# First projections of a hybrid transformer layer: fp32 matmuls over all tokens become three fp32r passes over two token halves

## The reference, cut to what matters

```python
qa, ka, va, za, aa, ba, ub, qn, kn, vn, gr = split_cols(h @ w_in)
...
qkv = jax.nn.silu(short_conv(jnp.concatenate([q, k, v], axis=-1), conv_w))
q = l2norm(q.reshape(b_, t_, GDN_HEADS, GDN_DK))
k = l2norm(k.reshape(b_, t_, GDN_HEADS, GDN_DK))
if rotary:
    q = axial_rope(q)
    k = axial_rope(k)
...
return (rmsnorm(o, norm_w) * jax.nn.silu(zh)).reshape(b_, t_, GDN_V_W)
```

## Time and profile before

| | |
|---|---|
| median of 3 runs | 3821.11 us |
| lowest, highest | 3817.90, 3821.98 us |
| the profiled execution: own time | 3825.0 us |
| its span | 3823.5 us |
| mean granted clock of TensorE | 0.977 |
| TensorE busy | 3659.4 us, 96% |
| VectorE, ScalarE, GpSimd busy | 2323.0, 1645.7, 856.0 us |

### The profile page before, as it was taken

How to read it: one execution, slowest core, us unless ns; L and a number is a source line. 1 busy time by engine, 2 the same in 40 slices (tenths; PEclk the granted TensorE clock), 3 DMA queues, 4 the chain that set the end, 5 groups by cost and what they waited for, 6 DMA issues and landing times. The chain is left out here.

```text
span 3823.5 us, 58042 instructions
## 1 busy us (share of the span) xinstructions
PE 3659.4 (96%) x19520; PEld 2936.9 (77%) x19520; DVE 2323.0 (61%) x3546; ACT 1645.7 (43%) x3006; POOL 856.0 (22%) x812
## 2 busy tenths in 40 slices
PE   8999999999997999989999999996799999999998
PEld 3444459986777999968888888785688888888887
DVE  4655632555656999953534353444767777677775
ACT  4333333334654666642424332322344445444452
POOL 3888500011106666610000000000000010000100
PEclk9999999999999999989999999997899999999999
DMA  7455455131115433344535352443477676766763
GB/s 283 155 144 142 119 182 130 57 86 45 26 46 183 125 118 122 96 160 125 177 105 170 99 172 73 152 154 130 145 214 226 214 220 206 214 224 215 219 209 92
DMA packets 258768, 570.97 MB, mean 149 GB/s; under 512 B 38971, under 2 KB 117339, under 8 KB 256347
## 3 DMA queue, kind: packets, MB, share of 16 engines
q1 hardware_dynamic: 225612, 451.18, 37.2%
q0 software_dynamic: 33040, 118.25, 10.4%
HBM read 458.27 MB, written 100.73 MB: 146 GB/s over the span
## 5 line engine op out<-in xcount | busy, mean ns | idle before, releaser
L3072 DVE TENSOR_TENSOR sb_we_low<-sb_we,sb_we_high 128x1024 fp32r<-128x1024 f32 x384 | 466.6, 1223 | 121.5 <-ACT sb_we_high L3023 121.5
L3023 ACT ACTIVATE sb_we_high<-sb_we 128x1024 fp32r<-128x1024 f32 x377 | 392.2, 1048 | 142.3 <-PE ey L2987 142.3
L2430 DVE TENSOR_TENSOR sb_wm_low<-sb_wm,sb_wm_high 128x1024 fp32r<-128x1024 f32 x127 | 155.4, 1224 | 393.6 <-ACT sb_wm_high L2340 393.6
L344 PE MATMUL p_ps<-sb_hT,sb_ring 128*128 128x512 f32 (+1 forms) x960 | 373.2, 549 | 0.0
L344 PEld LDWEIGHTS p_ps<-sb_hT,sb_ring 128*128 128x128 f32 x960 | 181.9, 190 | 186.2 <-issue 181.3
L2281 PE MATMUL pg<-sb_hb_high,sb_wm_high 128*128 128x512 f32 x768 | 303.3, 395 | 8.7 <-DVEq L2402 4.6
L2282 PE MATMUL pg<-sb_hb_low,sb_wm_high 128*128 128x512 f32 x768 | 300.4, 391 | 0.0
L2283 PE MATMUL pg<-sb_hb_high,sb_wm_low 128*128 128x512 f32 x768 | 300.1, 391 | 0.0
L2970 PE MATMUL eg<-sb_xe_parts,sb_we_high 128*128 128x512 f32 x1024 | 260.5, 396 | 1.6 <-DVE sb_xe_parts L3067 1.6
L2970 PE MATMUL eu<-sb_xe_parts,sb_we_high 128*128 128x512 f32 x1024 | 259.1, 395 | 0.0
L2932 POOL DMA_INDIRECT out<-sb_ybe,sb_ti x32 | 51.0, 1595 | 880.7 <-DVE sb_ybe L3107 822.7
(11 more groups left out here) (418 smaller groups left out, 8675.7 us busy)
## 6 DMA issues: line engine op xcount, KB each, us to landing
sb_we<-in_w_ex SPq DMA_DIRECT2D x384, 512.0 KB, 4.5
sb_wm<-in_w_gates SPq DMA_DIRECT2D x96, 512.0 KB, 3.6
sb_stage<-in_w_mod_row POOLq DMA_DIRECT2D x64, 256.0 KB, 3.6
sb_stage<-h_d SPq DMA_DIRECT2D x32, 512.0 KB, 4.3
sb_wm<-in_w_br SPq DMA_DIRECT2D x32, 512.0 KB
sb_ring<-in_w_ch POOLq DMA_DIRECT2D x19, 512.0 KB, 5.2
sb_gr<-gc_d SPq DMA_DIRECT2D x36, 256.0 KB, 3.8
sb_lk<-k_d SPq DMA_DIRECT2D x36, 256.0 KB, 4.0
```

The costliest lines, as they stand in the source:

```text
L344: last = nc.tensor.matmul(ps[:, b % BANKS, 0:wd], w[:, kind, k], hT[:, k, t0:t0 + wd], start=(k == 0), stop=(k == KD - 1))
L2430: v.tensor_tensor(wl[n], w[n], wh[n], ALU.subtract).then_inc(s.wl, 1)
L3023: nc.scalar.activation(wh[:, n % CUT], w[:, n % RAW], ACT.Copy).then_inc(s.wh, 1)
L3072: v.tensor_tensor(wl[:, n % CUT], w[:, n % RAW], wh[:, n % CUT], ALU.subtract).then_inc(s.wl, 1)
```

## The change

**Projection.** The tokens are taken in two halves of 1152 (`OWN`), 1154 with the neighbours of the convolution. Each of the 14 tiles is done once per half: 28 half tiles p = 0 to 27, in the order q, k, v of heads 0 to 3, two gates, and again for the second half. `hx` holds the high and low part of one half of the normed tokens, `wx` those of two weight tiles; a block's product is three fp32r matmuls per channel group. Blocks are 256, 450, 448 (first half), 386, 384, 384 (second); gates 448, 448 in the first half.

**Splitting.** High parts are ScalarE copies (`high_rows`, `high_weight`), low parts VectorE subtractions (`low_rows`, `low_weight`; one weight tile per half tile). Squares, norm and affine step of the second half's tokens are spread over half tiles 3 to 13, with their sums on TensorE in p = 4, 5, 7, 8, 11, 12; one third of these rows goes to DRAM and is loaded again at the turn from p = 13 to 14.

**Order.** In step p TensorE projects p, and after its first block does the sums of p-2 (before: of t-1) and the transposes of p-4 (before: t-2); VectorE does the convolution of p-1 whole, the norm of p-2, the low weight of p+1, the rotation of p-3 (before: t-2). Squares go to `rs`, no longer to `cv`. `stores` keeps its order within a head. GpSimd's 64 row parts go three to a half tile, p = 3 to 23.

```diff
-                    for k in range(KD):
-                        last = nc.tensor.matmul(ps[:, b % BANKS, 0:wd], w[:, kind, k], hT[:, k, t0:t0 + wd],
-                                                start=(k == 0), stop=(k == KD - 1))
+                    if b == 0:
+                        pe.wait_ge(s.wl, p + 1)
+                    if p in (0, NP // 2):
+                        need = max(n for n, (at, _) in enumerate(SPLITS) if at < off + wd)
+                        pe.wait_ge(s.hl, 2 * (NBK * half + need + 1))
...
+                    for k in range(KD):
+                        high, low = (wx[:, p % 2, part, k * P:(k + 1) * P] for part in range(2))
+                        rh, rl = (hx[:, part, k, off:off + wd] for part in range(2))
+                        nc.tensor.matmul(bank, high, rh, start=(k == 0), stop=False)
+                        nc.tensor.matmul(bank, high, rl, start=False, stop=False)
+                        last = nc.tensor.matmul(bank, low, rh, start=False, stop=(k == KD - 1))
...
@@ TensorE, step p
+                    for b in range(len(BLKS[p])):
+                        project(p, b)
+                        if b == 0 and two:
+                            sums(*two[0:2], (0, 1))
+                        if b == 0 and four:
+                            transpose(*four[0:2], (0, 1))
+                        if b == 0 and two:
+                            sums(*two[0:2], (2,))
+                        if b == 1 and four:
+                            transpose(*four[0:2], (2,))
+                        if b == 1 and p == NP - 1:
+                            transpose(*stage(NP - 4)[0:2], range(NG))
+                        if b == 0 and p in (4, 7, 11):
+                            norm_sums(NBK + (4, 7, 11).index(p), (0, 1))
+                        if b == 0 and p in (5, 8, 12):
+                            norm_sums(NBK + (5, 8, 12).index(p), (2, 3))
+                transpose(*stage(NP - 3)[0:2], range(NG))
...
@@ ScalarE, step p
+                    if 0 < p < NP - 1:
+                        high_weight(p + 1)
+                    evict(p, 0)
+                    if two:
+                        logs(*two[0:2])
+                        reciprocal_roots(*two[0:2])
+                    if four:
+                        copy_turned(*four[0:2], (0, 1))
...
+                    if one:
+                        activate(*one[0:3])
+                    evict(p, 1)
+                    if four:
+                        copy_turned(*four[0:2], (2,))
...
+                    for b in range(2, nb):
+                        evict(p, b)
+                    if one and one[1] < 2:
+                        squares_of(*one[0:2])
...
@@ VectorE, step p
                     if one:
-                        convolve(*one, (0, 1))
+                        convolve(*one)
                     if two:
-                        norm(*two)
-                    if one:
-                        convolve(*one, (2, 3, 4))
-                    if two:
-                        rotate(*two)
+                        norm(*two[0:2])
+                    if 0 < p < NP - 1:
+                        low_weight(p + 1)
+                    if p == NP // 2:
+                        low_rows(NBK + 2)
+                    if three:
+                        rotate(*three[0:3])
+                    if p in (7, 10, 13):
+                        normalise(NBK + (7, 10, 13).index(p))
...
@@ GpSimd
+                for p in range(3, NP):
+                    load_weight(p)
+                    if p in (7, 10, 14):
+                        add_squares(NBK + (7, 10, 14).index(p), (0, 1))
+                    if p in (8, 11, 15):
+                        add_squares(NBK + (8, 11, 15).index(p), (2, 3))
...
+                    if first <= p < last:
+                        for i in range(ROWP * (p - first) // (last - first), ROWP * (p + 1 - first) // (last - first)):
+                            row_part(i)
```

More of the change, by code:

```diff
@@ L346, in project, with sums @@
                     last.then_inc(s.proj, 1)
-                def sums(h, kind):
-                    r = 2 * h + kind
+                def sums(hh, kind, blocks):
+                    r = 2 * hh + kind
                     pe.wait_ge(s.sq, r + 1)
-                    for b, (t0, wd) in enumerate(BLOCKS):
-                        wait(pe, s.root, NB * r + max(b - 1, 0))
-                        nc.tensor.matmul(pn[:, b % 2, 0:wd], g.ones, cv[:, t0:t0 + wd], start=True, stop=True).then_inc(s.sum, 1)
@@ L355, in transpose @@
-                def transpose(h, kind):
-                    m = 2 * h + kind - 1
+                    if r == 0:
+                        pe.wait_ge(s.nln, NBK)
+                    for b in blocks:
+                        t0, wd = SUMS[b]
+                        wait(pe, s.root, NBK * r + max(b - 1, 0))
+                        nc.tensor.matmul(pn[:, b % 2, 0:wd], g.ones, rs[:, t0:t0 + wd], start=True, stop=True).then_inc(s.sum, 1)
+                def transpose(hh, kind, groups):
+                    m = 2 * hh + kind - 1
@@ L382, in mod_columns @@
                     last.then_inc(s.colt, 1)
-                def norm_sums(b):
-                    wd = BLOCKS[b][1]
-                    wait(pe, s.nln, b - 1)
-                    for j in range(2):
-                        pe.wait_ge(s.nadd, 2 * b + j + 1)
-                        for i in range(2):
-                            last = nc.tensor.matmul(pn[:, b % 2, 0:wd], g.ones, sqr[:, j, i, 0:wd],
-                                                    start=(j == 0 and i == 0), stop=(j == 1 and i == 1))
-                        last.then_inc(s.nsumh, 1)
@@ L436, in _, with norm_sums @@
[L436 removed]
+                def norm_sums(i, js):
+                    wd = SPLITS[NORMS[i][1]][1]
+                    bank = pn[:, i % 2, 0:wd] if i < NBK else pr[:, 0:wd]
+                    wait(pe, s.nln, i - 1 if i < NBK else i)
+                    for j in js:
+                        pe.wait_ge(s.nadd, 4 * i + j + 1)
+                        nc.tensor.matmul(bank, g.ones, squared(i, j)[:, 0], start=(j == 0), stop=(j == 3)).then_inc(s.nsumh, 1)
+                mod_rows()
@@ new lines, in _ @@
+                pe.wait_ge(s.cst, 16)
+                norm_sums(0, range(4))
+                mod_columns()
+                for i in range(1, NBK):
+                    norm_sums(i, range(4))
+                for p in range(NP):
+                    two, four = stage(p - 2), stage(p - 4)
+                    two = two if two and two[1] < 2 else None
+                    four = four if four and four[1] > 0 else None
+                    for b in range(len(BLKS[p])):
[14 more added lines that the diff above has]
+                            norm_sums(NBK + (5, 8, 12).index(p), (2, 3))
@@ L634, in window @@
+                normalise(0)
+                low_weight(0)
+                low_rows(0)
+                normalise(1)
+                low_rows(1)
+                normalise(2)
+                low_rows(2)
+                low_weight(1)
+                dve.wait_ge(s.cvw, 16)
+                for p in range(NP):
+                    one, two, three = stage(p - 1), stage(p - 2), stage(p - 3)
                     two = two if two and two[1] < 2 else None
+                    three = three if three and three[1] < 2 else None
+                    if p == NP // 2:
+                        low_rows(NBK)
+                        low_rows(NBK + 1)
```

709 lines of the change are left out of this document (382 added, 327 removed).

## The result

| | before | change |
|---|---|---|
| median of 4 runs | 3821.55 us | 3882.23 us |
| lowest, highest | 3817.90, 3825.34 | 3879.13, 3887.36 |
| ratio | | 1.016 (95%: 1.0142 to 1.0178) |
| span of the profiled execution | 3823.5 us | 3881.4 us |

What follows compares the result with a forecast made beforehand. The prediction took TensorE as the bound, with GpSimd nearly full. Its terms, -83 + 28 + 20 + 13 + 6 + 27 + 18 + 8, gave +37 and a forecast of 3858 us, range 3803 to 3898.

Steps and rivals of the forecast that it cites:

- Saving: First-stage projections on TensorE: passes of more even width shorten tiles and gate tiles, 83 us less.
- Head stalls: TensorE waits for a low weight behind the late q swap and rotation, heads 1 to 3 each half: 28 us.
- Third sum: The third block of sums waits for the first log with two PSUM banks: 1.25 us for each of 16, 20 us.
- First half tile: At the start TensorE waits for VectorE to prepare each further third of the rows: 13 us.
- GpSimd: Row parts and additions of the second half's squares come late for TensorE: 6 us over six places.
- The turn: Between the halves, a 35 us chain of stores, swaps, rotations, norm and splitting leaves TensorE waiting: 27 us.
- End: Last half tile and stage end: k transposes delayed 13 us, 5 added to the gap before the next stage: 18 us.
- Clock: TensorE's lower granted clock after some six long stalls, 2 us lost after each, partly covered: 8 us.
- rival 2: Contention makes VectorE and GpSimd the bound in the changed stage: 3899 us, chance 15%.
- Rival 1: The swap's transfer is hidden, so head stalls shrink or vanish and the kernel is faster: 3787 us, chance 15%.
- Rival 3: Stalls and saving cancel, half of the stalls being covered: about -5 to +5, 3821 us, chance 10%.

Runs made afterwards that it cites:

- swap_early: The change, with SP issuing the swaps of q and k ahead of its waits for transposes and the store of q; 3823.41 us.
- no_row_arith: The change without the scaling and addition of GpSimd's row parts, so their product is missing; 3861.99 us.
- warm: The change, with TensorE's stalls filled by matmuls whose result nobody reads; 3882.43 us.
- third_bank: Kernel both, with the third block of sums in another PSUM bank wherever that one is free; 3800.82 us.
- both: The change with the early swap order of swap_early and the work at the turn between the halves reordered; 3811.26 us.
- rows_spread: third_bank with GpSimd's row parts dealt out anew over the half tiles and half tile 12's third sum later; 3809.16 us.

## Why the prediction was right, and where it was off

The sign, the mechanism and the place were right; the size came out as near as it did with some luck, since terms that were too large hid others that were too small. Point by point, forecast and measured:

- *Saving, -83:* 426.3 us of passes before; a group of three passes of 384 columns takes 0.53 us (422.19 to 425.89 in 7 groups, 176 ns a pass instead of 174), of 450 columns 0.62 (206 instead of 202). That makes 12.7 us a half tile and 350 in all: -76. Sums and transposes, which I left at their size, gave 7 more.
- *Head stalls, +28:* 32.2 in the four. The chain read v copied at 15.0, measured 15.2 after the half tile's start; store 1.7; swap issue 3.9 instead of 2.5, at a DMA share of 0.72 (180 to 188 us) and not 0.59 (496 to 503 before); landed 24.2 instead of 22; low weight done at 37.8 instead of 34.6.
- *Third sum, +20:* 8.0, of it 6.3 in the eight tiles of the first half and 1.7 in those of the second. The first log runs no earlier than I had it (168.47, 5.4 us into half tile 6), but the transposes stand between the second and the third block, which leaves a wait of 0.89 us there; and in the second half the block ahead of the sums has 386 columns instead of 256, so that the log is early enough. I counted neither.
- *First half tile, +13:* gaps of 7.9 and 2.4, less 1: 9.
- *GpSimd, +6:* the one wait for its additions is 1.02 (134.11). The waits of 2.44 and 4.22 at half tiles 9 and 12 end with VectorE's low weight, and were in no term: VectorE comes late out of the swap's wait and then, from 187.3 to 222.6 us, works without a pause, with the norm and affine step of the second half's rows (6.8 us from 204.0) ahead of the next convolution. Both waits for the low weight are gone in swap_early and in no_row_arith.

```profile
222.63 0.48 PE L434 MATMUL p_ps<-sb_hq,sb_wq 128*128 128x256 f32 x1 [2.44 <-DVE sb_wq L734]
...
204.00:222.60 18.60, 16.19 (x79) 13.65 (x78) 18.42 (x15) 10.46 (x18) 13.36 (x10) 0.95 0.31 88
```

- *The turn, +27:* 41.1, the largest miss. The chain was right in its order, but read 35 us and took 42.5 (307.84 to 350.31), and TensorE was idle for 35.9 of it, where I had taken 27, the low end of my own 27 to 31. The swap of q was issued in 4.6 us instead of 2.5 and landed 10.2 after that instead of 4, beside the stores and reloads that the turn itself causes (share 0.87 from 309 to 325 us). And I left out its second part: the reload, which SP issues only at 350.3, behind both swaps and its own wait for the first low rows, makes TensorE wait 5.2 again for the last third of the rows.
- *End, +18:* 12.05, 3.88 and 2.8 more at the mixer: 18.8. The tail of 5 was 6.7, the delay of k's transposes 12 instead of 13.
- *Clock, +8:* the passes took 381 us against 350. Of these 31 us 12.4 vanish with the stalls in swap_early; 18 stay in every version that keeps the three passes and were in no term. Some 5 of them lie in the first two half tiles (the clock is 0.68 from 50 to 80 us). Most of the rest is in the first group of a block that stands behind sums and transposes or behind a pause: 0.91 us instead of 0.62 (103.70 to 104.61). Why these groups are slow at a clock of 1.00 no run shows. What the clock behind a stall costs in the end, warm puts at nothing.

The sum of the measured terms is -83 + 32 + 8 + 9 + 1 + 7 + 41 + 19 + 31 = 65. A wait of 1.3 us (447.84) stands in no term, and 4.7 us of short pauses of the kernel before are gone; that makes 61.3 within the rounding. The forecast's 37 lacked 14 in the turn, 23 in the clock (18 of it in passes that no stall slows), 7 at half tiles 9 and 12 and 4 in the head stalls. It had 12 too many in the third sum, 5 in GpSimd's and 4 in the first half tile; without these 21 it would have missed by 45 instead of 24.

Two readings were off without bearing on the sum. VectorE's 36 to 38 us in three half tiles are 34 to 36 by the terms given; in third_bank it works 33.4 us in three where GpSimd does little (443.3 to 487.1), and 39.6 in three on the average of 352.5 to 487.1. And GpSimd's 91 of the earlier trace rows are us of 102, 89%, where rival 2 reads them as per cent.

```profile
422.19 0.34 PE L434 MATMUL p_ps<-sb_hq,sb_wq 128*128 128x384 f32 x1
...
425.89 0.34 PE L434 MATMUL p_ps<-sb_hq,sb_wq 128*128 128x384 f32 x1
...
103.70 0.66 PE L434 MATMUL p_ps<-sb_hq,sb_wq 128*128 128x450 f32 x1
104.61 0.37 PE L434 MATMUL p_ps<-sb_hq,sb_wq 128*128 128x450 f32 x1
```

**The rivals.** Rival 1 (the swap is hidden) was wrong for the change, where v's transposes are copied at 15.2 us and not at 11.5. It was also too hopeful about what a hidden swap gives: in swap_early, where it is hidden, the kernel takes 3823 us, as before the change, and not 3787. Rival 3 (stalls and saving cancel, 3821) had half of the stalls covered; the head stalls and the turn came out larger than the forecast instead. The Trainium skill's advice in "DMA: Bandwidth & Descriptors", section "Rules for kernel authors", to issue early and wait late, agrees with swap_early once both halves of it are kept; the change kept the second only. Rival 2 (contention) was wrong as a bound: GpSimd waited 98 us for VectorE's low weights in this window, and no_row_arith gave 20 us. Its premise held, that an instruction loses the same however long it is:

```profile
L744 DVE SCALAR_TENSOR_TENSOR sb_cv<-sb_raw,sb_cw,sb_cv 128x1154 f32<-128x1154 f32 x25 | 52.4, 2096 | 0.9
...
L744 DVE SCALAR_TENSOR_TENSOR sb_cv<-sb_raw,sb_cw,sb_cv 128x1152 f32<-128x1152 f32 x24 | 34.0, 1419 | 0.8
```

The first group is from 81 to 194 us, with GpSimd busy, the second from 476 to 580, with GpSimd quiet: 0.68 us lost in each, against 0.59 in one of twice the width (3.23 and 2.64). I had taken half. The Trainium skill, "SBUF — State Buffer", section "Who interferes with whom", has the later instruction wait for the whole of the earlier; with that, the loss doesn't shrink with the width, and the trace agrees.

## What to carry to other kernels

When work is moved a step later to give a transfer time, look at what the transfer's issue stands behind on its queue: here the reader came a step later and the issue with it, and one reordering of a DMA queue was worth 59 us. Follow the longest chain through every engine it crosses in order, and reckon each transfer with the load that the chain's own neighbours put on the queues. And once the old bound is relieved, ask how far the next engine is behind: here VectorE was at 86%, so that of some 200 us of further TensorE work taken away only 25 came back.

## What the hardware showed that was not expected

- The issue of a DMA on SP, 0.59 us in the median, held SP for 7.69 us at 246.90 in both and for 9.40 us at 304.92 in rows_spread, while the DMA engines were full (share 1.05 and 1.02 in these stretches). What stands behind it on that queue is issued only then.
- A stall filled with matmuls that nobody reads kept the granted clock at 1.00 (0.65 without them) and left the kernel's time as it was.
